# A streaming encoder step on one core: attention scores with two heads' queries as one 128-column stationary operand

## The reference

```python
sq = rope(rmsnorm(sq.reshape(b, l, SWA_HEADS, SWA_HD), q_norm_g), pos)
sk = rope(rmsnorm(sk.reshape(b, l, SWA_KV_HEADS, SWA_HD), k_norm_g), pos)
# chunks of c = 64 queries; band = 128 earlier keys and the chunk's 64; 16 meta keys; a sink per head
s_meta = einsum('bnqkgd,mkd->bnkgqm', qb, meta_k) * d ** -0.5
s_band = einsum('bnqkgd,bnskd->bnkgqs', qb, kb) * d ** -0.5
p = softmax(concatenate([s_meta, s_band, sink], -1), -1)
o = einsum('bnkgqm,mkd->bnqkgd', p_meta, meta_v) + einsum('bnkgqs,bnskd->bnqkgd', p_band, vb)
```

## Time and profile before

| | |
|---|---|
| median of 3 runs | 568.24 us (564.68 to 569.65) |
| span of the profiled execution | 563.3 us |
| PE busy | 501.6 us, 89% |
| VectorE (DVE) busy | 262.0 us, 47% |
| GpSimd (POOL) busy | 156.9 us, 28% |
| ScalarE (ACT) busy | 131.4 us, 23% |
| moved by DMA | 144.75 MB, 257 GB/s over the span |

### The profile page before, as it was taken

The page is one execution under the profiler, slowest core; times in us unless marked ns, Lnnn a source line. Parts: engine busy times, 40 slices in busy tenths (PEclk is TensorE's granted clock), DMA queues, the critical chain, the costliest instruction groups (busy, mean ns, idle before and its releaser), DMA issues.

```text
span 563.3 us, 7848 instructions
## 1 busy us (share of the span) xinstructions
PE 501.6 (89%) x2907; PEld 318.3 (57%) x2907; DVE 262.0 (47%) x593; ACT 131.4 (23%) x351; POOL 156.9 (28%) x279
## 2 busy tenths in 40 slices
PE   4976999899999999999994799979999869778984
PEld 4955877777777777778884654333333333333333
DVE  2859588767344565672226622322334221112535
ACT  4754343354546322232111100000000000000110
POOL 5446683042214554741104300211111220100003
PEclk9989999799999999999997699979999998889998
DMA  8440220040026832219949799999999999999997
GB/s 294 158 127 3 75 76 2 1 144 8 2 74 234 240 123 86 79 52 407 420 167 351 296 385 396 417 423 417 417 421 420 418 420 417 419 420 423 411 411 225
DMA packets 35031, 144.75 MB, mean 257 GB/s; under 512 B 5842, under 2 KB 8994, under 8 KB 23216
## 3 DMA queue, kind: packets, MB, share of 16 engines
q1 hardware_dynamic: 26320, 129.94, 58.8%
q0 software_dynamic: 4528, 9.01, 4.3%
q10 hardware_dynamic: 4144, 5.28, 2.9%
HBM read 138.16 MB, written 17.30 MB: 276 GB/s over the span
## 4 chain that ended last, share of the span: by engine, by line
PE 46%; DMA 18%; DVE 13%; SPq 10%; issue 4%; ACT 3%; POOL 1%; DVEq 0%; POOLq 0%; ACTq 0%
PE banks L1051 19%; SPq L715 7%; PE banks L1278 6%; DMA w_moe_b<-in_w_up_dram 5%; DMA y_d<-rows,idx 3%; DMA y_d<-y_sb,idx 3%; SPq L723 3%; DMA w_moe_b<-y_d 3%; PE banks L1109 3%; DMA y_d<-x_row,idx 2%; PE banks L1293 2%; PE banks L1045 2%; DMA y_sb<-hn_d,idx 2%; PE banks L1194 1%; PE banks L1189 1%
## 5 line engine op out<-in xcount | busy, mean ns | idle before, releaser
L872 POOL TENSOR_TENSOR w_lo<-w_raw,w_hi 128x512 fp32r<-128x512 f32 x52 | 70.6, 1371 | 119.6 <-ACT w_hi L1556 117.7
L1278 PE MATMUL banks<-w_moe_b,xgT 128*64 128x512 f32 x224 | 67.8, 626 | 9.6 <-DMA w_moe_b<-in_w_up_dram 6.6
L1278 PE MATMUL banks<-w_moe_a,xgT 128*64 128x512 f32 x224 | 69.0, 639 | 4.9 <-DMA w_moe_a<-in_w_up_dram 4.9
L2211 DVE SCALAR_TENSOR_TENSOR glu_b<-banks,wr,glu_a 128x256 f32<-128x256 f32 x15 | 7.2, 483 | 98.4 <-ACT glu_a L1680 98.4
L1680 ACT ACTIVATE glu_a<-banks,wr 128x256 f32<-128x256 f32 x15 | 7.1, 475 | 196.6 <-PE banks L1278 183.5
L1051 PE MATMUL banks<-w_hi,xT_hi_a 128*128 128x512 f32 (+3 forms) x124 | 50.5, 408 | 1.6 <-DVE xT_lo_a L1742 1.6
L1278 PEld LDWEIGHTS banks<-w_moe_b,xgT 128*64 128x64 f32 x224 | 21.1, 144 | 48.7 <-issue 45.7
L1051 PE MATMUL banks<-w_lo,xT_hi_a 128*128 128x512 f32 (+3 forms) x124 | 48.2, 388 | 0.0
L1051 PE MATMUL banks<-w_hi,xT_lo_a 128*128 128x512 f32 (+3 forms) x124 | 48.0, 387 | 0.0
L1278 PEld LDWEIGHTS banks<-w_moe_a,xgT 128*64 128x64 f32 x224 | 21.7, 146 | 27.6 <-issue 25.8
L1051 PE MATMUL banks<-w_hi,xT_hi_b 128*128 128x512 f32 (+3 forms) x92 | 35.7, 388 | 0.8 <-issue 0.8
(11 more groups left out here) (334 smaller groups left out, 934.2 us busy)
## 6 DMA issues: line engine op xcount, KB each, us to landing
w_moe_a<-in_w_down_dram SPq DMA_DIRECT2D x20, 1024.0 KB, 20.3
w_moe_a<-in_w_gate_dram SPq DMA_DIRECT2D x16, 1024.0 KB, 11.6
w_moe_a<-in_w_up_dram SPq DMA_DIRECT2D x16, 1024.0 KB, 13.9
w_moe_b<-in_w_gate_dram SPq DMA_DIRECT2D x14, 1024.0 KB, 17.1
w_moe_b<-in_w_up_dram SPq DMA_DIRECT2D x14, 1024.0 KB, 17.0
w_moe_b<-in_w_down_dram SPq DMA_DIRECT2D x10, 1024.0 KB, 25.8
w_raw<-in_w_in_dram SPq DMA_DIRECT2D x34, 256.0 KB, 4.1
y_d<-in_consts_dram SPq DMA_DIRECT2D x9, 512.0 KB, 10.8
```

The costliest lines, as they stand in the source:

```text
L872: nc.gpsimd.tensor_tensor(w_lo[:, s, :], w_raw[:, s, :], w_hi[:, s, :].bitcast(F32), ALU.subtract).then_inc(split, 1)
L1278: l = mm(acc[64 * e:64 * e + 64, u, :].rearrange("p (m f) -> p m f", m=2), xgT[:, xu, k, 64 * e:64 * e + 64], units(at_e[e], 2)[:, :, k * ...
```

## The change

A unit's rows are no longer queries alone but (head of the pair, query of a chunk): 64 queries of two heads fill 128 partitions. `score` puts two heads' queries as one 128-column stationary operand. The two key groups, which lie in the two halves of the 64-deep contraction rows, are multiplied in turn, each into its own bank; the two chunks of a tile are now the two column ranges of a bank. The order of units changes so that units 2j and 2j+1 are the two key groups of one head pair; PE's matmuls for both stand at the second one. The transposed queries are laid out as (head pair, chunk, head, query). The root is applied in `post` of SQ, with one more product, so `post` now waits for it (`qk_root`); it and `qT` come one slot later, except for the last tile's. The softmax loses the multiplication by the root and uses per-partition sinks (`sink_of`, made in `tables` by two small copies). Tail units are one chunk wide on 128 partitions.

```diff
-UNITS = [(t, g, hh) for t in ORDER for g in range(2) for hh in range(2)]
+UNITS = [(t, g, hh) for t in ORDER for hh in range(2) for g in range(2)]
...
-        behind[s + (4 if t == ORDER[-1] else 0)].append(("post", SQ, t))
-        after[s + (7 if t == ORDER[-1] else 2 if t < TAIL else 3)].append(("qT", t))
+        behind[s + (4 if t == ORDER[-1] else 1)].append(("post", SQ, t))
+        after[s + (7 if t == ORDER[-1] else 3 if t < TAIL else 4)].append(("qT", t))
...
-    u0 = done(SQ, ORDER[0]) + 5
-    starts = [u0 + n * 23 // 19 + (1 if n > 3 else 0) for n in range(len(UNITS))]
+    u0 = done(SQ, ORDER[0]) + 6
+    starts = [u0 + n // 2 * 2 * 23 // 19 + (1 if n > 3 else 0) for n in range(len(UNITS))]
     for n, s in enumerate(starts):
-        before[s + 1].append(("norm", n))
-        after[s + 3].append(("value", n))
+        before[s + 1 + n % 2].append(("norm", n))
+        after[s + 3 + n % 2].append(("value", n))
     for n, s in enumerate(starts):
-        after[s + 2].append(("pT", n))
+        after[s + 2 + n % 2].append(("pT", n))
...
+            pair_bank = {}
             def score(i, b):
                 t, g, hh = UNITS[i]
                 take(b)
+                pair_bank[g] = b
+                if g == 0:
+                    return
...
-                for hl in range(2):
-                    for lots in zip(*keys):
-                        for c2, (col, n, dst) in enumerate(lots):
-                            l = mm(sideA[64 * c2:64 * c2 + 64, b, 256 * hl + dst:256 * hl + dst + n],
-                                   sqT[gs, ORDER.index(t) % DEEP, 2 * hh + hl, CH * c2:CH * c2 + CH],
-                                   skT[gs, col:col + n], start=True, stop=True)
-                l.then_inc(s_ps, 1)
+                    for col, n, dst in lots:
+                        for kv in range(2):
+                            gs = slice(64 * kv, 64 * kv + 64)
+                            l = mm(sideA[:, pair_bank[kv], 256 * c2 + dst:256 * c2 + dst + n],
+                                   sqT[gs, ORDER.index(t) % DEEP, 2 * hh + c2, :],
+                                   skT[gs, col:col + n], start=True, stop=True)
+                l.then_inc(s_ps, 2)
...
+                step(tt(a, a, b, ALU.add))
+                dve.wait_ge(qk_root, nth["root", SQ, t])
+                r = rstd_qk[0:R, qk_cols(SQ, t)]
                 for g in range(2):
-                    l = tt(sq[0:R, i % 2, :, g, :], a[:, 4 * g:4 * g + 4, :], b[:, 4 * g:4 * g + 4, :], ALU.add)
+                    hs = slice(4 * g, 4 * g + 4)
+                    l = tt(sq[0:R, i % 2, :, g, :], a[:, hs, :], r[:, hs].unsqueeze(2).to_broadcast([R, 4, HD]), ALU.mult)
...
-                step(red(v[:, 0:2], s2[0:R, :, 0:KEYS], AX_X, ALU.max))
-                dve.wait_ge(qk_root, nth["root", SQ, t])
-                step(stt(out=v[:, 0:2], in0=v[:, 0:2], scalar=-1.0, in1=rstd_qk[0:R, QH * t + h:QH * t + h + 2],
-                         op0=ALU.mult, op1=ALU.mult))
-                step(tt(v[:, 2:4], v[:, 0:2], neg_sinks[0:R, h:h + 2], ALU.min))
-                tt(v[:, 6:8], sinks[0:R, h:h + 2], v[:, 2:4], ALU.add).then_inc(s_max, 1)
+                step(red(v[:, 0:nc2], s2[:, 0:nc2, 0:KEYS], AX_X, ALU.max))
+                step(ts(v[:, 2:2 + nc2], v[:, 0:nc2], -1.0, neg_sinks[:, u:u + 1], ALU.mult, ALU.min))
+                ts(v[:, 6:6 + nc2], v[:, 2:2 + nc2], sink_of[:, u:u + 1], None, ALU.add).then_inc(s_max, 1)
```

More of the change, by code:

```diff
@@ L233, in out_rows, with chunks_of @@
     return P if t < TAIL else DEC
+def chunks_of(t):
+    return out_rows(t) // CH
 def constants():
@@ L1111, in score @@
                                    skT[gs, col:col + n], start=True, stop=True)
-                l.then_inc(s_ps, 1)
+                l.then_inc(s_ps, 2)
             def probs_T(i, b):
-                R = out_rows(UNITS[i][0])
+                nc2 = chunks_of(UNITS[i][0])
                 q = i % DEEP
                 pe.wait_ge(s_prob, i + 1)
-                for hl in range(2):
-                    nc.tensor.transpose(sideA[:, b, hl * P:hl * P + R], probs[0:R, q, hl, 0:P], ident[0:R, 0:R])
@@ L1120, in probs_T @@
-                for hl in range(2):
-                    l = nc.tensor.transpose(sideA[0:CH + NMETA, b, 2 * P + hl * P:2 * P + hl * P + R],
-                                            probs[0:R, q, hl, P:KEYS], ident[0:R, 0:R])
+                for c2 in range(nc2):
+                    nc.tensor.transpose(sideA[:, b, c2 * P:c2 * P + P], probs[:, q, c2, 0:P], ident)
+                for c2 in range(nc2):
+                    l = nc.tensor.transpose(sideA[0:CH + NMETA, b, 2 * P + c2 * P:2 * P + c2 * P + P],
+                                            probs[:, q, c2, P:KEYS], ident)
@@ L1598, in score @@
                     act.wait_ge(pT_ps, i - DEEP + 1)
-                for hl in range(2):
-                    af(probs[0:R, q, hl, :], sideA[0:R, b, 256 * hl:256 * hl + KEYS], ACT.Exp,
-                       scale=rstd_qk[0:R, h + hl:h + hl + 1], bias=soft[0:R, q, 2 + hl:3 + hl],
-                       accum_out=soft[0:R, q, 4 + hl:5 + hl])
-                af(soft[0:R, q, 8:10], soft[0:R, q, 6:8], ACT.Exp).then_inc(s_exp, 1)
+                for c2 in range(nc2):
+                    af(probs[:, q, c2, :], sideA[:, b, 256 * c2:256 * c2 + KEYS], ACT.Exp,
+                       bias=soft[:, q, 2 + c2:3 + c2], accum_out=soft[:, q, 4 + c2:5 + c2])
+                af(soft[:, q, 8:8 + nc2], soft[:, q, 6:6 + nc2], ACT.Exp).then_inc(s_exp, 1)
             def probs_T(i, b):
-                R = out_rows(UNITS[i][0])
+                nc2 = chunks_of(UNITS[i][0])
                 q = i % DEEP
@@ L1771, in tables @@
                     dve.wait_ge(g_in, 16 * 5)
-                    step(ts(neg_sinks[:, :], sinks[:, :], -1.0, None, ALU.mult))
+                    for hl in range(2):
+                        half = slice(64 * hl, 64 * hl + 64)
+                        step(nc.vector.tensor_copy(sink_of[half, :], sinks[half, hl:QH:2]))
+                    step(ts(neg_sinks[:, :], sink_of[:, :], -1.0, None, ALU.mult))
                 else:
@@ L1916, in score @@
[L1916 to L1922 removed]
+                    nc.vector.memset(s2[:, 0, 0:WINDOW], NEG)
@@ L1927, in norm @@
+                v = soft[:, i % DEEP, :]
                 dve.wait_ge(s_exp, i + 1)
-                step(tt(v[:, 10:12], v[:, 4:6], v[:, 8:10], ALU.add))
-                step(nc.vector.reciprocal(v[:, 12:14], v[:, 10:12]))
-                tt(probs[0:R, i % DEEP], probs[0:R, i % DEEP], v[:, 12:14].unsqueeze(2).to_broadcast([R, 2, KEYS]),
-                   ALU.mult).then_inc(s_prob, 1)
+                step(tt(v[:, 10:10 + nc2], v[:, 4:4 + nc2], v[:, 8:8 + nc2], ALU.add))
+                step(nc.vector.reciprocal(v[:, 12:12 + nc2], v[:, 10:10 + nc2]))
@@ L1933, in value @@
+                p = probs[:, i % DEEP, 0:nc2, :]
+                tt(p, p, v[:, 12:12 + nc2].unsqueeze(2).to_broadcast([P, nc2, KEYS]), ALU.mult).then_inc(s_prob, 1)
             def value(i, b):
```

51 lines of the change are left out of this document (25 added, 26 removed).

## The result

The changed kernel takes 574.03 us, the kernel before on the same chip 567.25 us (median of 7 runs each, 570.33 to 578.01 and 564.68 to 569.65). The ratio is 1.013, interval 1.010 to 1.016: 1.3% slower, where 1.2% faster was forecast. Its profiled execution has a span of 574.9 us, against 563.3. The granted clock is 0.947 to 0.950 in the changed kernel's three shortest runs (570.33 to 572.20 us) and 0.936 to 0.939 in the other four, of which the profiled one (576.76 us) is one.

The account below looks back on a forecast made before the run. TensorE's stream was taken to bound the kernel up to about 300 us, the experts' weight stream after. Terms −8.0 + 1.8 − 0.8 + 0 = −7.0 us gave 561.2 us, 1.2% less, range 556.5 to 567.

Parts of the forecast that it names:

- What the matmuls cost: TensorE's score matmuls: full, tile 0 and tail pairs at 1.2, 1.05 and 0.85 us, saving 8.0 us.
- The sentence of the Trainium skill: Weight loads overlap running matmuls only when row_grp differs; as a rival it gave 567.0 us, chance 0.04.
- The moved wait: VectorE's `post` of SQ waiting for GpSimd's root would cost TensorE 1.8 us net, bounds 0 and 6.
- The three holes: TensorE's idle stops for the queries of tiles 4, 0 and later, put at 0.5, 3.6 and 0 us.
- the walk: Step-by-step timing of VectorE, GpSimd and TensorE from 48.35 us, and of VectorE's steps around 95 us.
- From there nothing of this reaches TensorE: After post(1), done at 67.0 us and wanted at 67.9, the moved wait would no longer idle TensorE.
- Around 95 us: VectorE reaches `norm` 5's end at 96.9 us; TensorE idles 1.8 instead of 2.6 us, 0.8 won.
- The clock: Slow-clock cost in the attention part taken as unchanged, 0 us, with 3.4 us on either side.
- The waits eat more: Rival: both holes bring 6.8 us slow stretches, or VectorE's stops continue through tiles 1 and 2; 564.7 us, chance 0.20.
- VectorE becomes the bound: Slower rival: every post SQ stands for its root, five stops of 3 us; 575 us, chance 0.08.
- the gain is made and given back in the experts: Rival: the time won before the experts is lost again in them; 568 us, chance 0.05.
- The link from TensorE to the weight stream: At 287 to 298 us, loads wait for TensorE's counts, so the experts' weight stream moves as much as TensorE does.

Follow-up runs that it names:

- e8: Changed kernel with the score loop over the two key groups moved outside that over the key ranges, same matmuls: 578.27 us in two runs, ratio 1.0217.
- e4: Changed kernel with the last tile's post of SQ one slot later, behind `norm` 5: 569.84 us, ratio 1.006.
- e9: Changed kernel with post SQ's wait and product split off a slot later, last post SQ one slot later, RQK posts six later: 564.92 us, ratio 0.9975.
- e11: Changed kernel with a constant for the root (no wait), last post SQ one slot later, RQK posts six later: 557.87 us, ratio 0.9861.
- e10: Kernel before with the last post SQ one slot later and the RQK posts six slots later: 560.29 us, ratio 0.9886.
- e5: Changed kernel with post SQ split, rotation and addition staying, wait and product one slot later except the last tile's: 572.80 us, ratio 1.013.

## Why the prediction was wrong, step by step

**What the matmuls cost: right.** 1.2, 0.85 and 1.05 us a pair were put, 1.21, 0.77 and 1.00 measured; 152 records, and the two halves of a pair start 7 ns apart. Saved 8.2 against 8.0, and 0.8 for the transposes that were left out. The twenty units of before sum to 19.0 us by the prediction's own costs, not 18.9; nothing hangs on it. The sentence of the Trainium skill ("TensorE: Matmul & The Clock Gate", What overlaps and what doesn't) that was weighed there doesn't hold for these loads. In the first 0.33 us of e8's tail pair one row half is at work alone, by the order in the program and the starts of the records. Its loads start at 69.927, 70.035 and 70.144, its matmuls at 69.928 and 70.142: the third load runs beside the second matmul, in the same row half.

**The moved wait: wrong in size, +1.8 put, +5.6 in the waits for `sq` alone (7.9 instead of 2.3).** The three holes were put at 0.5, 3.6 and 0 us and came at 2.2, 4.3 and 1.4. The sequence was right up to the end of the first root. All times of the walk move by 1.1 for the later start: the root was put at 53.9 and came at 54.1, VectorE's stop at 2.2 and was 2.55. Then "the products end at 53.6" (54.7): they ended at 56.08. The product was priced at 0.8 us, its time with a quiet GpSimd, although the same walk has "GpSimd has two weight lows first" right there. The price for this meeting stood in the earlier trace rows, 1176 ns on average for `rqk`'s product against 692 for an addition of the same shape, and was used around 95 us, but not here. It stood in before's own timeline too, in the 1.83 us of the additions at 53.93. The copy of `v_own` met the second low (+1.0). So the sums were 2.4 us late (they ended at 58.7 instead of 56.3), GpSimd's root started 2.1 us late, and the next product collided as before's had: 65.31 instead of 61.7. From tile 4's sums to the end of tile 0's products the walk has 12.9 us (47.75 to 60.6); 16.5 were measured, and three of the missing 3.6 are these three meetings, one each.

"From there nothing of this reaches TensorE" fell for the same reason. VectorE did reach the post of SQ(2) with its root ready, but two weight lows lay on its rotation:

```profile
82.90 2.97 POOL L877 TENSOR_TENSOR w_lo<-w_raw,w_hi 128x512 fp32r<-128x512 f32 x2 [0.18 <-POOL rstd_qk L303]
83.01 1.72 DVE L1819 TENSOR_TENSOR h_a<-sq,rope_gq 128x512 f32<-128x512 f32 x1
84.77 1.38 DVE L1820 TENSOR_TENSOR h_b<-sq,rope_gq 128x256 f32<-128x256 f32 x1
86.19 0.43 DVE L1821 TENSOR_TENSOR h_b<-sq,rope_gq 128x256 f32<-128x256 f32 x1
```

1.72 and 1.38 instead of 0.69 and 0.43: 2.0 us, and TensorE stands 1.44 us from 86.84.

**"Around 95 us": −0.8 put, the holes grew.** The walk had 12.1 us for VectorE from the two scores to `norm` 5. It took 14.3, from 95.8 to 110.1. Missing were 1.4 us in which VectorE stood for ScalarE's `mix_hi`, and 1.0 us because not one weight low but two lay on post RQK(0) (5.0 us instead of 4.0). The hole is 4.41 us, one of 1.35 at 134 us comes on top. e4 shows that the place of post SQ(3) is part of this, e9 and e11 that the place of post RQK is the rest: with both moved, the waits for `probs` are 1.0 us.

**The clock: 0 put, +5.6.** "I take the sum as unchanged" was a guess with ±3.4 on it. Four stretches took the place of one. In part they go with the holes: where a run removed them, these stretches went too (e10 has none between 44 and 181 us). But how many stretches a hole brings stays open: e4 keeps two of the holes without theirs, and e10 has one without a hole at 181.9 us. And at least the one at 57.6 us, 1.7 of the 5.6, cost nothing, as e4 shows.

**The rivals.** "The waits eat more" named the right thing, "VectorE's stops go on through tiles 1 and 2", and priced it with 3 to 4 us on top of the forecast's +1.0; idle time and clock came to 14.7. The slower rival, "VectorE becomes the bound", has the right time (575), which is in part luck, as the mechanism is partly another: not five stops of 3 us but two of 2.5 and one of 1.4, and VectorE's work stretched where it meets GpSimd. "By my walk it has 1 to 2 us to spare there" is the sentence that decided its chance, and it used up those 2 us in one rotation. Both were treated as alternatives, though they are one case at two sizes. That "the gain is made and given back in the experts" didn't occur: the kernel came to them 6.4 us late. The link from TensorE to the weight stream was right: DMA's share of 0.33, in before from 287 to 298 us, stands 6.4 us later in the changed kernel, from 293.4 to 304.4.

## What to carry to other kernels

When an engine is made to wait for another, price what both do in the moment after: the end of the wait starts them together, and what had queued behind the producer falls on the consumer. A gain in the bounding engine's stream is worth its size only while each feeder keeps its lead; here the lead was worth more than the matmuls, and moving two unhurried steps in the old kernel brought 1.1% without touching a matmul. And if a walk leaves 1 to 2 us to spare on an engine that has just worked 11.46 of 12 us, do it again with the collided durations before giving the other case 8 in 100.

## What the runs showed of the hardware

**VectorE and GpSimd take turns.** A VectorE instruction with two SBUF inputs that starts while a weight low of GpSimd (two inputs too) runs ends after the low, by its own length less some 0.14 us: by 0.02 us if alone it takes 0.15 (128x1), by 0.28 if 0.42 (128x256), by 0.55 if 0.69 (128x512). So between 50 and 105 us 128x512 takes 1.63 to 1.72 us, 128x256 takes 1.38 to 1.49, and 128x1 takes 0.94. One that starts ahead of the low keeps its length (the first of the two products at 54.26 takes 0.42 us), and the low is drawn out, from 1.28 to between 1.39 and 1.84 us; GpSimd's small steps go from 0.20 to between 0.31 and 0.65. A reduction with one input isn't touched:

```profile
76.62 2.54 POOL L877 TENSOR_TENSOR w_lo<-w_raw,w_hi 128x512 fp32r<-128x512 f32 x2 [5.83 <-ACT w_hi L1566]
...
77.63 0.69 DVE L1839 TENSOR_REDUCE ssq_qk<-squares 128x8 f32<-128x512 f32 x1 [1.15 <-ACT squares L1544]
78.23 0.94 DVE L1940 TENSOR_TENSOR soft<-soft 128x1 f32<-128x1 f32 x1
```

The copy of `v_own`, one input in SBUF, is held as well (1.66 us instead of 0.68 in e5). This is read from coincidence in the timelines of all kernels here; no run took the lows away. The Trainium skill ("GPSIMD Engine Reference", Specifications) has the two sharing their SBUF interfaces, with contention for VectorE instructions with two SBUF inputs or in a two-port mode; the rows agree. In them VectorE's instruction waits for the whole rest of GpSimd's.

**The slow clock often follows short holes.** Holes of 1.44, 2.21, 4.26 and 4.41 us were followed, or overlapped, by 3.4, 3.4, 6.8 and 6.8 us at the 1.2 GHz level. It isn't a rule for one hole: in the earlier trace rows, stops of 1.6 and 2.2 us left it at 1.00, and in e4 the same holes of 1.45 and 2.21 us were followed by no slow stretch, where after's were. Nor does each stretch need a hole: the one of 3.4 us at 181.9 in e10 comes behind 12 us with TensorE at work for 11.61.

**Loads hide behind matmuls of their own row half.** A full pair costs 1.21 us with the row halves alternating and 1.22 with four records of one half in a row; a tail pair 0.77, and 1.10 with six in a row, where the second half starts 0.33 us late.
